# A two-layer hybrid diffusion backbone on one core: layer 1's norm, attention and chunk order changed, and an opening with turns two blocks ahead

## The reference

```python
hx = modulate(rms_norm(x, g_mix[l]), sh1, sc1)        # shift and scale from adaln(c, w_ada[l])
hc = modulate(rms_norm(ctx, g_mix[l]), csh1, csc1)    # the same weights with c_ctx
px = split_cols(hx @ w_in[l], IN_SIZES)               # q k v | conformer | short conv | fourier | 4 gates
y_attn = windowed_latent_attention(q, k, v, kc, vc, sink)
x = x + gt1 * mixer_output(px, y_attn, ...)           # four branches, gated, summed, one projection
x = x + gt2 * conv_ffn(modulate(rms_norm(x, g_ffn[l]), sh2, sc2), w_up[l], ...)
```

## Time and profile before

| | |
|---|---|
| runs | 1308.24, 1308.53, 1309.39 us (median 1308.53) |
| profiled execution | 1308.54 us, span 1306.8 us |
| mean granted clock of TensorE | 0.991 |
| busy: PE, DVE, ACT, POOL | 96%, 68%, 42%, 22% |
| first matmul, first product of a chunk | 13.62 us, 24.66 us |
| TensorE busy in the first 60 us | 42.4 us |

### The profile page before, as it was taken

The page is one execution under the profiler, slowest core; times in us unless marked ns, Lnnn a source line. Parts: engine busy times, 40 slices in busy tenths (PEclk is TensorE's granted clock), DMA queues, the critical chain, the costliest instruction groups (busy, mean ns, idle before and its releaser), DMA issues.

```text
span 1306.8 us, 20012 instructions
## 1 busy us (share of the span) xinstructions
PE 1260.5 (96%) x7718; PEld 1092.8 (84%) x7718; DVE 884.4 (68%) x1205; ACT 550.9 (42%) x872; POOL 291.7 (22%) x247
## 2 busy tenths in 40 slices
PE   4999999999999999999999999989989998999997
PEld 3788777777788798888888888989878998999997
DVE  4698678753699777662889664475676666665654
ACT  4322255553423245331223342344566645643543
POOL 0003699210233001111001110003871230220220
PEclk8999999999999999999999999999999998999999
DMA  9466311222366425662646663245333543664560
GB/s 376 155 224 201 121 61 61 73 65 76 108 201 242 124 71 183 190 216 76 205 161 195 195 216 134 66 125 174 114 105 100 194 160 130 200 217 139 183 209 33
DMA packets 50339, 198.76 MB, mean 152 GB/s; under 512 B 5584, under 2 KB 6992, under 8 KB 49104
## 3 DMA queue, kind: packets, MB, share of 16 engines
q1 hardware_dynamic: 50256, 197.62, 45.9%
HBM read 196.55 MB, written 1.05 MB: 151 GB/s over the span
## 4 chain that ended last, share of the span: by engine, by line
PE 84%; DVE 9%; ACT 4%; issue 2%; DMA 0%; SPq 0%; DVEq 0%; ACTq 0%
PE psA L522 24%; PE psA L524 24%; PE psA L523 24%; DVE w_lo L1268 2%; ACT w_hi L958 2%; PE psB L522 2%; PE psB L524 2%; PE psB L523 2%; DVE acc L1549 2%; DVE small L1562 1%; PE psA L773 1%; PE psB L801 1%; PE psB L789 1%; PE psB L704 1%; PE psB L543 1%
## 5 line engine op out<-in xcount | busy, mean ns | idle before, releaser
L522 PE MATMUL psA<-h_hi,w_hi 128*128 128x256 f32 (+1 forms) x1544 | 523.7, 339 | 10.1 <-DVE w_lo L1268 4.0
L524 PE MATMUL psA<-h_hi,w_lo 128*128 128x256 f32 (+1 forms) x1544 | 516.8, 335 | 0.0
L523 PE MATMUL psA<-h_lo,w_hi 128*128 128x256 f32 (+1 forms) x1544 | 516.7, 335 | 0.0
L1268 DVE TENSOR_TENSOR w_lo<-raw,w_hi 128x1024 fp32r<-128x1024 f32 (+2 forms) x244 | 336.3, 1378 | 124.3 <-ACT w_hi L958 124.2
L958 ACT ACTIVATE w_hi<-raw 128x1024 fp32r<-128x1024 f32 (+2 forms) x244 | 277.1, 1138 | 297.6 <-PE psA L524 226.6
L522 PEld LDWEIGHTS psA<-h_hi,w_hi 128*128 128x128 f32 x1544 | 295.2, 191 | 43.9 <-issue 7.0
L524 PEld LDWEIGHTS psA<-h_hi,w_lo 128*128 128x128 f32 x1544 | 295.3, 191 | 29.1
L523 PEld LDWEIGHTS psA<-h_lo,w_hi 128*128 128x128 f32 x1544 | 295.4, 191 | 27.9 <-issue 0.2
L511 POOL TENSOR_TENSOR hid_lo<-sig,hid_hi 128x512 f32 (+3 forms) x44 | 66.8, 1519 | 475.5 <-ACT hid_hi L1233 475.5
L1289 DVE SCALAR_TENSOR_TENSOR ada_sum<-raw,csil,ada_sum 128x1024 f32<-128x1024 f32 x112 | 155.8, 1421 | 0.0
L522 PE MATMUL psA<-hid_hi,w_hi 128*128 128x256 f32 (+1 forms) x352 | 116.3, 330 | 2.1 <-DVE sig L1742 2.0
(11 more groups left out here) (194 smaller groups left out, 1484.0 us busy)
## 6 DMA issues: line engine op xcount, KB each, us to landing
raw<-w_up SPq DMA_DIRECT2D x88, 512.0 KB, 4.2
raw<-w_ada SPq DMA_DIRECT2D x80, 512.0 KB, 3.6
raw<-w_dn SPq DMA_DIRECT2D x32, 704.0 KB, 4.5
raw<-w_in SPq DMA_DIRECT2D x36, 512.0 KB, 4.2
raw<-w_at SPq DMA_DIRECT2D x24, 512.0 KB, 3.5
raw<-w_fn SPq DMA_DIRECT2D x16, 640.0 KB, 3.9
raw<-w_sc SPq DMA_DIRECT2D x16, 640.0 KB, 3.8
raw<-w_cf SPq DMA_DIRECT2D x16, 640.0 KB, 4.0
```

The lines of the kernel that those rows point to most:

```text
L522: pe.matmul(out, w0, hi, start=first, stop=False)
L523: pe.matmul(out, w0, lo, start=False, stop=False)
L524: return pe.matmul(out, w1, hi, start=False, stop=last)
L1268: dve.tensor_tensor(w_lo[:, s, 0:tiles * P], raw[:, r, 0:tiles * P], w_hi[:, s, 0:tiles * P].bitcast(F32), ALU.subtract).then_inc(rest_don ...
```

## The change

It touches the opening, the order of the "in" chunks in both layers, the norm at the entry of layer 1 and VectorE's order in layer 1's attention.

- **Opening.** The constants' load moves behind the first quarter of x. The loads come in the order first 0, w_in 0, first 1, w_in 1, first 2, w_in 2, first 3, w_in 3, first 4 to 7. The table for the root is loaded before the squares. TensorE issues six idle matmuls when the second quarter of x is there and two more before the second turn. Row products and turns run two blocks ahead: in block c the row product c + 2 stands behind chunk 0's product and the turn c + 2 behind chunk 2's. `FIRST_LAG` becomes 0, 1, 2, 3. VectorE takes the shift of block c + 1 before the rest of h of block c. GpSimd splits chunks 2 and 3.
- **"in" chunks.** The order is q (4), Fourier (2), short conv (6), k, v, conformer (4). Rotations stand behind chunks 5, 6, 7, 8 and (for k) 14, the Fourier channels behind chunk 10, the positions behind 12, v's transposes behind 15. One reduction of the shift vectors moves to chunk 16.
- **Entry of layer 1.** The context half of the norm goes one tile per step into steps 0 to 7. k and v are done on all 512 columns.
- **Attention of layer 1.** VectorE takes `peak` before `rest`, and `weight_sum` before the second tap.

```diff
-FIRST_LAG = [0, 0, 1, 2]
+FIRST_LAG = [0, 1, 2, 3]
-REDUCE = {ADA_START[_g] + 10 + (4 <= _g < 8): _g for _g in ADA_START}
+REDUCE = {START["in"] + 16 if _g == 2 else ADA_START[_g] + 10 + (4 <= _g < 8): _g for _g in ADA_START}
-SPLIT_IN_NORM = {0: 0, 2: 1, 4: 2}
+ROT_AT = {5: 0, 6: 1, 7: 2, 8: 3, 14: 4}
...
-            sp.dma_start(mat[:, 0:MAT["rot"]], io["mat"][:, 0:MAT["rot"]]).then_inc(mats_in, 16)
+                if j == 0:
+                    sp.dma_start(mat[:, 0:MAT["rot"]], io["mat"][:, 0:MAT["rot"]]).then_inc(mats_in, 16)
...
-                for n in ([0, 1], [2], [3])[c] if c < 3 else []:
-                    sp.dma_start(raw[:, n, 0:KD * P], io["w_in0"][n]).then_inc(raw_full[n], 16)
+                if 1 <= c <= FIRST_LEAD:
+                    sp.dma_start(raw[:, c - 1, 0:KD * P], io["w_in0"][c - 1]).then_inc(raw_full[c - 1], 16)
...
+            for n in range(2, FIRST_LEAD):
+                pool.wait_ge(head_done, n + 1)
+                pool.wait_ge(rest_done, n)
+                pool.tensor_tensor(w_lo[:, n, 0:KD * P], raw[:, n, 0:KD * P], w_hi[:, n, 0:KD * P].bitcast(F32),
+                                   ALU.subtract).then_inc(rest_done, 1)
...
-                pool.wait_ge(evac, n0 + 14)
+                pool.wait_ge(evac, n0 + 12)
...
+            def keep_warm(count):
+
+                for _ in range(count):
+                    pe.matmul(psA[3][:, 0:SEQ], glu[:, 0, 0, 0:P], glu[:, 0, 0, 0:SEQ], start=True, stop=True)
+
+            pe.wait_ge(pads, 1)
+            pe.wait_ge(x_full[1], 16)
+            keep_warm(6)
...
+            pe.wait_ge(csil_done, 1)
+            first_product(0)
             pe.wait_ge(inv, 2)
...
-            pe.wait_ge(csil_done, 1)
-            first_product(0)
             turn_first(0)
+            first_product(1)
+            keep_warm(2)
+            turn_first(1)
             for at_ in range(KD + max(FIRST_LAG)):
-                if at_ + 1 < KD:
-                    first_product(at_ + 1)
                 if at_ < KD:
                     pe.wait_ge(h_rest, 2 * (at_ + 1))
...
-                    if j == 0 and at_ + 1 < KD:
-                        turn_first(at_ + 1)
+                    if j == 0 and at_ + 2 < KD:
+                        first_product(at_ + 2)
+                    if j == 2 and at_ + 2 < KD:
+                        turn_first(at_ + 2)
...
-                    pe.wait_ge(rope, 15 * (layer + 1))
-                    pe.wait_ge(v_done, layer + 1)
+                    pe.wait_ge(rope, 15 * layer + 12)
+                    pe.wait_ge(evac, n0 + 6)
...
+                    both_streams = idx in (12, 13)
+                    if both_streams:
+                        pe.wait_ge(h_rest, 32 * layer + 16)
+                    cols = NT if both_streams else T
...
+                        if j == 4:
+                            pe.wait_ge(fn_rest, fc0 + 2 * streams(layer))
...
+            early_table(ACT.Sqrt)
...
+            first_row_out(0)
+            head(Step(-AHEAD, 0), 8)
+            first_row_out(1)
+            for c in range(KD):
                 for s in range(2):
...
+                if c + 1 < FIRST_LEAD:
+                    head(Step(c + 1 - AHEAD, 0), 8)
+                if c + 2 < KD:
+                    first_row_out(c + 2)
...
+                    if layer and idx < KD:
+                        shifted_head(layer, 0, 1, idx)
...
+            rest(Step(-AHEAD, 0), 8)
+            first_shift(0)
+            dve.wait_ge(spread, 2)
+            for c in range(KD):
...
+                if c == 1:
+                    rest(Step(1 - AHEAD, 0), 8)
+                if c + 1 < KD:
+                    first_shift(c + 1)
                 for s in range(2):
...
                     dve.wait_ge(h_head, 2 * c + s + 1)
...
-                if c < 2:
-                    rest(Step(c + 2 - AHEAD, 0), 8)
...
-                    if st.n and not (layer and idx in SPLIT_IN_NORM.values()):
+                    if st.n:
                         rest(st, size(st, "in"))
+                    if layer and idx < KD:
+                        if idx == 0:
+                            dve.wait_ge(spread, normed(2, 1))
+                        scaled(layer, 0, 1, idx)
...
+                    if layer and idx < KD:
+                        shifted_rest(layer, 0, 1, idx)
...
-                    if 6 <= idx < 11:
+                    if idx in ROT_AT:
...
                     def step(st):
+                        k = at_place(layer, place, 0) if place is not None else None
+                        if k is not None and layer:
+                            peak(k)
                         rest(st, size(st, name))
...
+                            if layer and place % 2:
+                                weight_sum(place // 2)
                             if 2 * place + 1 < CONF_K:
                                 conv_tap(2 * place + 1)
...
-                        if place is not None and layer and place % 2:
-                            weight_sum(place // 2)
```

More of the change, by code:

```diff
@@ L222, in program @@
         root_col = place("root_col", [NT // P])
+        spare = place("spare", [1])
         ada_part = place("ada_part", [2, P * KD // 32])
@@ L1012, in norm @@
                     norm_root(r, 0)
-                for s in range(norm_streams(r)):
-                    cols = slice(s * SEQ, (s + 1) * SEQ)
+                for s in range(norm_streams(r) - (r == 2)):
                     for kk in range(KD):
-                        if r == 2 and s == 1 and kk in SPLIT_IN_NORM:
-                            head(Step(PER_LAYER + SPLIT_IN_NORM[kk], SPLIT_IN_NORM[kk]), SIZE[AHEAD])
                         if norm_streams(r) > 1 and s == 0 and kk == 2:
@@ L1039, in _, with first_row_out @@
                 act.activation(buf[:, 0:NT], X[:, kk, 0:NT], ACT.Square).then_inc(first_sq, 1)
-            early_table(ACT.Sqrt)
-            act.wait_ge(stat, 2)
-            act.activation(root_col[:, :], psB[0][:, 0:4], ACT.Sqrt, bias=V("eps", 0)).then_inc(root, 2)
-            for ahead in range(2):
-                head(Step(ahead - AHEAD, 0), 8)
-            for c in range(KD):
-                if 1 <= c <= 2:
-                    head(Step(c + 1 - AHEAD, 0), 8)
+            def first_row_out(c):
                 act.wait_ge(first_mm, c + 1)
@@ L1448, in _, with first_shift @@
             op.then_inc(inv, 2)
-            for ahead in range(2):
-                rest(Step(ahead - AHEAD, 0), 8)
-            dve.wait_ge(spread, 2)
-            for c in range(KD):
+            def first_shift(c):
                 dve.wait_ge(first_turn, c + 1)
@@ L1514, in _ @@
                                           ALU.mult).then_inc(evac, 1)
-                    elif idx in (12, 13):
-                        dve.tensor_copy(pb(layer, idx - 12), ps[:, 0:T]).then_inc(evac, 1)
-                    else:
+                    elif idx in (10, 11):
+                        dve.tensor_copy(pb(layer, idx - 10), ps[:, 0:T]).then_inc(evac, 1)
+                    elif idx == 12:
+                        dve.tensor_copy(k_all[:, :], ps[:, :]).then_inc(evac, 1)
+                    elif idx == 13:
+                        dve.tensor_copy(tmp[1][:, :], ps[:, :]).then_inc(evac, 1)
+                    elif idx in (15, 17):
                         c = (idx - 15) // 2
@@ L1537, in _ @@
                         dve.tensor_tensor(dst, dst, tmp[j % 2][:, 0:SEQ], ALU.add).then_inc(rope, 1)
-                    ada_behind(st)
+                    if layer == 0:
+                        ada_behind(st)
                 def conv_tap(j):
@@ L1593, in step @@
                                 conv_tap(2 * place)
-                            k = at_place(layer, place, 0)
-                            if k is not None:
+                            if k is not None and layer == 0:
                                 peak(k)
```

132 lines of the change are left out of this document (51 added, 81 removed).

## The result

The changed kernel took 1302.3 us as the median of five runs, against 1308.84 us for the kernel before beside it: a ratio of 0.9928, with a 95% interval from 0.9902 to 0.9955. The median is the forecast to the tenth. That agreement is luck: the gain in the layers and the loss in the opening were both sized too small, and the errors cancelled. The five runs lie in two groups, 1296.42 and 1297.85 us with a mean granted clock of 0.995 and 0.994, and 1302.3, 1302.49 and 1303.51 us with 0.992. The profiled run is the one of 1296.42 us, so its rows must be read as those of the upper clock.

A forecast was written before the change was run, and what follows sets the result against it. TensorE, busy 1260.5 us or 96% of the span, was taken as the bound. Attention, opening, k and v, and entry summed as 1308.5 - 5.6 + 3.0 - 0.6 - 3.0 = 1302.3 us, range 1298.0 to 1307.5.

The forecast's parts named there:

- Attention, 5.6 forecast: Layer 1's attention: peak before the chunk split and sum before the second tap remove waits of 3.1 and 2.5 us.
- the rival that the attention keeps its waits: Layer 1's attention: VectorE, waiting for scores, delays its merge and splits, so nothing is gained there; 1307.9 us, chance 0.12.
- Entry and in part, 3.6 forecast: Layer 1's entry: spreading the norm gains 3.0 us after new rotation waits; k and v on 512 columns gain 0.6.
- Layer 0, whose new order was forecast at nothing: Layer 0's chunk order: costs nothing, since chunks and the operations of VectorE and ScalarE stay the same.
- The opening at full clock, 0.5 slower forecast: Opening: first product 3.2 us earlier at 21.5, but waits and longer stagger make it 0.5 us slower even at full clock.
- The clock, 2.5 forecast: Opening, new blocks 0 and 1: a low-clock stretch of 6.8 us costs 2.5 us.
- the rival in which the clock stays high: Opening: idle matmuls raised the clock and no wait exceeds 2 us, so it stays up; 1299.8 us, chance 0.22.
- The two splits on GpSimd: Opening: splits of 2.9 us on GpSimd against 1.23 on VectorE, covered because chunks are wanted 5 us after their copies.
- The rival in which the idle matmuls don't raise the clock: Opening: statistic, product 0 and spread keep their old length, 1.9 us later; 1304.2 us, chance 0.08.
- the slower rival: Opening: low clock holds itself, each such block costing 3.6 us more; five blocks give 1317.8 us, chance 0.06.

The follow-up runs named there:

- the kernel with filled waits: Changed kernel with two idle matmuls of 192 columns ahead of the waits for h_lo of the opening's first four blocks: 1297.37 us, ratio 0.9921.
- the entry alone: Kernel before with only the new chunk order and the new entry of layer 1, opening and attention as before: 1302.89 us, ratio 0.9963.
- the early sum alone: Kernel before with only the sum of the weights and its reciprocal ahead of the second tap in layer 1's attention: 1303.1 us, ratio 0.9964.

## Why the prediction was right, and what was wrong in it

The forecast was 9.2 us less in the layers and 3.0 more in the opening. Measured apart, the layers give 12.2 us (7.1 + 5.1; both in one kernel, with the old opening, 10.9) and the opening costs 4.4; the sum is 7.8 (6.5 with the 10.9), and the changed kernel's median was 6.5 and 6.3 us under the kernel before.

**Attention, 5.6 forecast, 7.1 alone and 6.9 by milestones.** The mechanism was right: the peak stood behind a split and a tap, and both waits for prob vanished. That the two causes add up, 3.1 and 2.5, was not: the halves overlap. The term was too small because it left out a third wait of the same chain, the 0.5 for probT, and some 0.8 that no wait of TensorE shows; where those were is open. That VectorE keeps up in spite of 9.3 of 10.5 us was right, so the rival that the attention keeps its waits is out.

**Entry and in part, 3.6 forecast, 3.4 by milestones.** Step by step: no wait for w_lo, rotation waits of 1.44 + 0.18 where the text had 1.4 + 0.6, a wait of 0.6 before the channels where it had 0.9, and a clock of 1.00 behind it. It sized this well.

**Layer 0, whose new order was forecast at nothing, gained 1.7.** This is what makes 5.1 of the 3.4. In VectorE's groups of layer 0's attention, the same operation on 128x2 elements took, in the changed kernel,

```profile
L1582 DVE SCALAR_TENSOR_TENSOR small<-small,nsink 128x2 f32<-128x2 f32 x16 | 6.8, 427 | 0.6
```

and in the kernel with filled waits, which has the same code there but the waits of 0.9 and 0.4 for prob,

```profile
L1584 DVE SCALAR_TENSOR_TENSOR small<-small,nsink 128x2 f32<-128x2 f32 x16 | 8.2, 512 | 0.5
```

The mean moves by 85 ns over 16 operations while GpSimd does its taps beside them. So the 1.7 us are not simply the new order's: by these rows they come and go with when VectorE's small operations meet GpSimd's. Of the fourteen profiles of this study, both of the changed kernel and the one of the entry alone are free of these waits, while six others with the same new order have them; the one with the early sum alone has 0.3 us, and the kernel before and nine others, these six among them, have 0.9 to 1.0 and 0.4 to 0.9 us. That it is the lock described above is likely by the sizes (0.16 or up to 1.26 us for one operation), but no run took GpSimd's taps away, so it is argued and not shown.

**The opening at full clock, 0.5 slower forecast; 0.2 slower found** by the first rotation (71.81 against 71.63 with the old opening). First product at 21.71 for 21.5; blocks of 4.38, 4.48 and 5.18 for 4.4, 4.6 and 5.3. The named cause, the turn stuck behind the third chunk and VectorE's rest of h behind the shift that waits for it, is shown by the run that takes that order away: of 6.6 us in seven waits 1.3 in two are left. Between the blocks the waits come to 5.8 us, 0.50 of it for the copy of a row, where the text had 2.0, 1.6 and four times 0.8, together 6.8.

**The clock, 2.5 forecast, 5.0 found** (5.4 between the two profiles, less the 0.4 by which x came later). This is the term that was mis-sized, by two of its sentences. "I take a low stretch as long as the one before, 6.8 us" was right in length when it came (6.9), but by the times it came in 9 of the changed kernel's 14 runs, with one more between (1299.22): the rival in which the clock stays high is the other 4, and it took 1296.4 to 1297.9 rather than 1299.8, because of the 1.7 to 3 us that the layers gave more and the opening's 0.3. It also came later, from 27 to 38 us, not from 20 to 33. And "about 70% of it is TensorE work on the chain, half of that lost" was too little for TensorE, whose slower work cost 3.1, and took the chain to be TensorE's alone. The other 1.9 sit in "The two splits on GpSimd [...] covered". They are covered for TensorE, which wants the chunks 5 us later (and take 2.4 us each, not 2.9), but VectorE's h_lo is not safe from them: shifted by the low clock, it meets the second split and takes 2.75 us instead of 0.87, and the block's wait grows from 1.29 to 3.17.

**The rival in which the idle matmuls don't raise the clock** is out: statistic 1.02 us. Without them it would have been 8.4 us, not the 1.9 that the rival was priced at. There the clock was up once (the second row product takes 1.07 us at 19.89), fell before the first product at 23.36 and stayed low to 36 us; the rival counted only the statistic, product 0 and the spread. Nor did any run go the way of **the slower rival**: in the changed kernel the clock rose again in block 2 and stayed up, as argued against it. The run without idle matmuls, whose low stretches reach beyond 40 us, shows that its mechanism exists.

## What to carry to other kernels

When an engine's next task waits for a partner that waits in turn for the task after it, look at which of two ready operations stands first: here turning two of VectorE's operations round was worth more (9.8 us, clock included) than the whole new opening, which cost 4.4. Price a low clock by the whole chain that it shifts, not by TensorE's work alone, and see from several runs whether it always comes; if it comes and goes, filling TensorE's short waits with idle matmuls can take the scatter out (here 1297.1 to 1298.4 instead of 1297.7 to 1304.1); where the waits were short already it gave nothing. Before work is moved to GpSimd, look which operations of VectorE with two SBUF inputs stand on the critical path beside it.

## What the hardware showed unexpectedly

- One program ran at two speeds. Its two profiles are 5.6 us apart, and of these 5.0 go with a granted clock that fell behind TensorE's waits of 1.29 us in the opening. The two profiles have the same waits up to the fall (1.29, 0.50 and 1.29); why it falls in one run and not in another stays open.
- GpSimd's split of 128x1024 elements took 2.34 to 2.47 us, and each of the three times that an h_lo had still to begin beside it, VectorE stood still for about two microseconds (2.75, 3.00 and 2.95 instead of 0.87), while a VectorE operation with an operand in PSUM ran beside it unchanged.
- Eight matmuls that compute nothing were worth 8.4 us to this kernel.
- The low stretch cost 3.1 us in one profile and 5.0 in another at the same length, 6.8 and 6.9 us: the difference is one meeting of h_lo with GpSimd.
